# Second attention by groups of two head pairs, third attention's masks added on the vector engine

## What is computed

```python
def forgetting_attention(q, k, v, fcum):          # second attention, 16 heads of 64
    logits = einsum('bhtd,bhsd->bhts', q * scale, k) + fcum[:, :, :, None] - fcum[:, :, None, :]
    p = softmax(where(causal, logits, -inf), axis=-1)
    return einsum('bhts,bhsd->bhtd', p, v)

def sliding_window_gqa(q, k, v, sinks):           # third attention, 16 query heads, 2 key heads, window 128
    s = einsum('bqhgd,bkhd->bhgqk', q, k) * scale
    s = where(band, s, -inf)
    m = maximum(max(s, axis=-1), sink)
    p = exp(s - m)
    return einsum('bhgqk,bkhd->bqhgd', p / (sum(p, -1) + exp(sink - m)), v)
```

## Time and profile before

| | us |
|---|---|
| time before, median of 3 runs | 879.39 (879.27 to 879.51) |
| the profiled execution's own time | 879.21 |
| its span in the trace | 877.5 |
| PE busy | 864.6 (99%) |
| DVE busy | 676.3 (77%) |
| ACT busy | 515.6 (59%) |
| granted TensorE clock, mean | 0.999 |
| second attention, first logits to last outs | 350.76 to 425.03 |
| third attention, first logits to last outs | 657.5 to 723.4 |

### The profile page before, as it was taken

One profiled execution on the slowest core, in us unless ns is written; L12 is line 12 of the kernel. 1 busy time (PEld: TensorE's weight loads), 2 busy tenths in 40 slices (PEclk: granted clock), 3 DMA queues, 4 the chain that ended last, 5 costly groups with the idle time before them and its releaser, 6 DMA issues.

```text
span 877.5 us, 15051 instructions
## 1 busy us (share of the span) xinstructions
PE 864.6 (99%) x5840; PEld 754.4 (86%) x5840; DVE 676.3 (77%) x942; ACT 515.6 (59%) x754; POOL 50.3 (6%) x86
## 2 busy tenths in 40 slices
PE   8999999999999999999999999999999999999997
PEld 8999889888888899888798888888888778998885
DVE  5766469888888986656589888879878877699684
ACT  6655657765655774555486655656736757542452
POOL 3910000000000010000010000000100001000000
PEclk9999999999999999999999999999999999999999
DMA  8553425555455445242456365354353333562321
GB/s 295 205 174 139 145 96 204 204 199 206 170 193 201 154 164 218 103 144 96 145 204 239 145 217 207 151 204 179 110 209 138 104 140 121 189 212 89 133 97 49
DMA packets 21977, 144.64 MB, mean 165 GB/s; under 512 B 2831, under 2 KB 3103, under 8 KB 5280
## 3 DMA queue, kind: packets, MB, share of 16 engines
q1 hardware_dynamic: 20448, 139.47, 44.3%
q0 software_dynamic: 1328, 4.32, 1.5%
q10 hardware_dynamic: 144, 0.04, 0.0%
HBM read 142.78 MB, written 1.05 MB: 164 GB/s over the span
## 4 chain that ended last, share of the span: by engine, by line
PE 88%; DVE 6%; issue 2%; ACT 1%; DMA 1%; POOL 0%; SPq 0%; DVEq 0%; POOLq 0%; ACTq 0%
PE psC L1937 15%; PE psC L1848 12%; PE psC L1849 11%; PE psC L1850 11%; PE psC L1940 8%; PE psD L1848 5%; PE psD L1849 4%; PE psD L1850 4%; PE psC L1967 2%; PE psC L1969 2%; PE psC L1976 2%; PE psD L2224 2%; DVE arena L1257 2%; PE psD L2201 1%; PE psD L2213 1%
## 5 line engine op out<-in xcount | busy, mean ns | idle before, releaser
L1060 DVE TENSOR_TENSOR w_lo<-raw,w_hi 128x2048 fp32r<-128x2048 f32 x125 | 285.8, 2288 | 54.3 <-ACT w_hi L528 53.6
L528 ACT ACTIVATE w_hi<-raw 128x2048 fp32r<-128x2048 f32 x125 | 238.5, 1912 | 71.4 <-PE psC L1850 44.1
L1937 PE MATMUL psC<-xT,w_hi 128*128 128x512 f32 x640 | 200.8, 395 | 0.0
L1940 PEld LDWEIGHTS psC<-xT,w_lo 128*128 128x128 f32 x640 | 120.2, 188 | 28.3
L1940 PE MATMUL psC<-xT,w_lo 128*128 128x256 f32 x640 | 125.7, 278 | 0.0
L1937 PEld LDWEIGHTS psC<-xT,w_hi 128*128 128x128 f32 x640 | 98.6, 189 | 1.2
L1848 PE MATMUL psC<-xT,w_hi 128*128 128x256 f32 x320 | 92.1, 288 | 0.0
L1849 PE MATMUL psC<-xT,w_hi 128*128 128x256 f32 x320 | 90.5, 283 | 0.0
L1850 PE MATMUL psC<-xT,w_lo 128*128 128x256 f32 x320 | 90.5, 283 | 0.0
L1848 PE MATMUL psD<-w_hi,oT_hi 128*128 128x512 f32 x208 | 81.4, 391 | 0.6 <-DVE oT_lo L1271 0.6
L1849 PE MATMUL psD<-w_lo,oT_hi 128*128 128x512 f32 x208 | 81.0, 390 | 0.0
(11 more groups left out here) (327 smaller groups left out, 1522.3 us busy)
## 6 DMA issues: line engine op xcount, KB each, us to landing
raw<-stream SPq DMA_DIRECT2D x130, 1024.0 KB, 4.8
gbc<-post_g POOLq DMA_DIRECT2D x6, 512.0 KB, 4.5
h<-x_in SPq DMA_DIRECT2D x2, 512.0 KB, 4.5
raw<-stream SPq DMA_DIRECT2D x4, 256.0 KB, 6.3
out<-h SPq DMA_DIRECT2D x3, 256.0 KB, 2.0
arena<-b_in POOLq DMA_DIRECT2D x1, 640.0 KB, 5.9
out<-h SPq DMA_DIRECT2D x2, 128.0 KB, 2.0
pv<-pvec POOLq DMA_DIRECT2D x1, 176.0 KB, 5.0
```

Of the source, the lines that this page charges most:

```text
L528: nc.scalar.activation(w_hi[:, slot, :], raw[:, raw_slot, :], ACT.Copy).then_inc(hi_done, 1)
L1060: V.tensor_tensor(w_lo[:, slot, :], raw[:, raw_slot, :], w_hi[:, slot, :].bitcast(F32), ALU.subtract).then_inc(lo_done, 1)
L1937: MM(psC[:, up_bank(e, a), :], hi[:, k, a * P:a * P + P], xT[:, kk_, :, :].rearrange("p i t -> p (i t)"), start=(kk_ == 0), stop=False, sk ...
L1940: ins = MM(psC[:, up_bank(e, a), 0:T], lo[:, k, a * P:a * P + P], xT[:, kk_, 0, :], start=False, stop=(kk_ == KT - 1), skip_group_check=True)
```

## The change

In the second attention, PE's work is put in a row for groups g of two pairs: the forget sums and masks of both pairs (`forget_rows`), the outs of the group before (`outs_group`, now in banks that both pairs of a group share, by `group_out`), the logits of both pairs; and later both transposes. ACT and DVE follow: two maxima, two exponentials, two normalisations in a row, and one copy of 512 columns for the outs of a group where two of 256 were.

In the third attention the two mask matmuls of each pair are gone. The first L2224 matmul of a bank opens it (`start`). DVE reads logits from PSUM and the mask from SBUF, adds them, writes the sum to `pair_p` and takes the maximum, in four `tensor_tensor_reduce`. The exponentials read `pair_p` in place of PSUM.

```diff
@@ pair_exps (ACT)
-                if p >= 3:
+                if p >= 3 and w == 0:
                     act.wait_ge(s["turned"], p - 2)
                 for r in range(2):
                     i = 2 * p + r
                     for q, (a, b) in enumerate(((0, P), (P, 384))):
-                        ins = nc.scalar.activation(pair_p[p % 3][:, r, a:b], psD[:, 2 * (p % 2) + r, a:b], ACT.Exp,
+                        z = pair_p[p % 3][:, r, a:b] if w else psD[:, 2 * (p % 2) + r, a:b]
+                        ins = nc.scalar.activation(pair_p[p % 3][:, r, a:b], z, ACT.Exp,
                                                    bias=nmx[:, w, i, q:q + 1], accum_out=sums[:, w, i, q:q + 1])
@@ fox (ACT)
-                for p in range(H // 2):
-                    if p:
-                        probs_turned(0, p - 1)
-                    pair_exps(0, p)
-                    split_to(u0 + p + 5)
-                    if p:
-                        out_hi(p - 1)
-                    if p % 2 == 0:
-                        values_evac(p // 2)
-                probs_turned(0, 7)
-                out_hi(7)
+                for g in range(4):
+                    if g:
+                        out_hi(g - 1)
+                    pair_exps(0, 2 * g)
+                    pair_exps(0, 2 * g + 1)
+                    values_evac(g)
+                    split_to(u0 + 2 * g + 5)
+                    probs_turned(0, 2 * g)
+                    probs_turned(0, 2 * g + 1)
+                    split_to(u0 + 2 * g + 6)
+                out_hi(3)
@@ pair_max (DVE)
                 dve.wait_ge(s["logit"], p + 1)
-                V.tensor_reduce(mx[:, w, pair, 0], psD[:, at:at + 2, 0:P], AX.X, ALU.max)
-                settle(V.tensor_reduce(mx[:, w, pair, 1], psD[:, at:at + 2, P:384], AX.X, ALU.max))
                 if w == 0:
+                    V.tensor_reduce(mx[:, w, pair, 0], psD[:, at:at + 2, 0:P], AX.X, ALU.max)
+                    settle(V.tensor_reduce(mx[:, w, pair, 1], psD[:, at:at + 2, P:384], AX.X, ALU.max))
                     V.tensor_scalar(nmx[:, w, pair, :], mx[:, w, pair, :], -1.0, None, ALU.mult).then_inc(s["max"], 1)
                     return
+                if p >= 3:
+                    dve.wait_ge(s["turned"], p - 2)
+                for r in range(2):
+                    for q, (a, b) in enumerate(((0, P), (P, 384))):
+                        ins = V.tensor_tensor_reduce(pair_p[p % 3][:, r, a:b], psD[:, at + r, a:b], mask_window[:, a:b], 1.0, NEG,
+                                                     ALU.add, ALU.max, accum_out=mx[:, w, 2 * p + r, q:q + 1])
+                settle(ins)
@@ fox (DVE)
-                for p in range(H // 2):
-                    pair_max(0, p)
-                    split_to(u0 + p + 4)
-                    if p in (1, 3, 5):
-                        fox_keys((p + 1) // 2)
-                    normalize(0, p)
-                    if p:
-                        out_lo(p - 1)
+                for g in range(4):
+                    pair_max(0, 2 * g)
+                    pair_max(0, 2 * g + 1)
+                    if g:
+                        out_lo(g - 1)
+                    split_to(u0 + 2 * g + 4)
+                    normalize(0, 2 * g)
+                    normalize(0, 2 * g + 1)
+                    if g < 3:
+                        fox_keys(g + 1)
+                    split_to(u0 + 2 * g + 5)
                 split_to(u0 + 12)
-                out_lo(7)
+                out_lo(3)
@@ fox (PE)
+                def forget_rows(g):
+                    for p in (2 * g, 2 * g + 1):
+                        if g:
+                            pe.wait_ge(s["pT"], p - 1)
...
-                for p in range(7):
-                    g = p // 2
-                    logits(p)
-                    if p:
-                        turn_probs(0, p - 1)
...
+                for g in range(4):
+                    forget_rows(g)
+                    if g:
+                        outs_group(g - 1)
+                    logits(g)
+                    vals(g, 2)
+                    vals(g, 3)
+                    if g == 3:
                         break
...
+                    for i in range(4):
+                        keys(g + 1, i)
+                    turn_probs(0, 2 * g)
+                    turn_probs(0, 2 * g + 1)
+                    vals(g + 1, 0)
+                    vals(g + 1, 1)
+                out_ready(3)
@@ window, logits(p) (PE)
-                    for z in zs:
-                        MM(z[:, 0:384], ident_b[:, :], mask_window[:, :], start=True, stop=False, skip_group_check=True)
-                    pair_logits(zs, p, p // 4).then_inc(s["logit"], 1)
+                    pair_logits(zs, p, p // 4, True).then_inc(s["logit"], 1)
```

More of the change, by code:

```diff
@@ L803, in fox, with out_hi @@
                 u0 = U0["fox_kv"]
-                def out_hi(p):
-                    act.wait_ge(s["out"], p + 1)
-                    nc.scalar.activation(oT_hi[:, p, :], psD[:, 2 * (p % 2), 0:T], ACT.Copy).then_inc(s["ohi"], 1)
+                def out_hi(g):
+                    act.wait_ge(s["out"], g + 1)
+                    nc.scalar.activation(oT_hi[:, 2 * g:2 * g + 2, :].rearrange("p k t -> p (k t)"), group_out(g), ACT.Copy).then_inc(s["ohi"], 1)
                 def values_evac(g):
@@ L2207, in outs @@
                 pe.wait_ge(s["pT"], p + 1)
-                if w == 0 and p % 2 == 0:
-                    pe.wait_ge(chunk_freed_s, S_FREED[E0["fox_kv"] + p + 1])
                 o = [psD[DH * r:DH * r + DH, 2 * (p % 2), 0:T] for r in range(2)]
-                first = [(p // 4 if w else 2 * p + r) * DH for r in range(2)]
+                first = [(p // 4) * DH for r in range(2)]
                 for r in range(2):
@@ L2217, in outs, with pair_logits @@
                 ins.then_inc(s["out"], 1)
[L2219 removed]
+            def pair_logits(zs, p, keys, opens=False):
                 for a, b, q in ((0, P, slice(0, P)), (P, 384, slice(P, T))):
@@ L2223, in pair_logits @@
                         rows = slice(DH * r, DH * r + DH)
-                        ins = MM(z[:, a:b], qT[rows, p, q], kT[rows, keys, 0:b - a], start=False, stop=(a > 0), skip_group_check=True)
+                        ins = MM(z[:, a:b], qT[rows, p, q], kT[rows, keys, 0:b - a], start=(opens and a == 0), stop=(a > 0),
+                                 skip_group_check=True)
                 return ins
@@ L2340, in vals, with out_ready @@
                     tokens_piece(e0 + 2 * g + 1, u0 + 2 * g + 1, part)
[L2342 to L2357 removed]
+                def out_ready(g):
+                    pe.wait_ge(s["olo"], g)
@@ new lines, in logit_banks @@
+                def logit_banks(p):
+                    return [psD[:, 2 * (p % 2) + r, :] for r in range(2)]
+                def forget_rows(g):
+                    for p in (2 * g, 2 * g + 1):
+                        if g:
+                            pe.wait_ge(s["pT"], p - 1)
+                        for r, z in enumerate(logit_banks(p)):
+                            MM(z[:, 0:384], sel_r[:, 2 * p + r, :], neg_f_all, start=True, stop=False, skip_group_check=True)
+                    for p in (2 * g, 2 * g + 1):
+                        for z in logit_banks(p):
+                            MM(diagonal(z), ident_b[:, :], diagonal(mask_causal[:, :]), start=False, stop=False, skip_group_check=True)
@@ new lines, in logits, with outs_group @@
+                def logits(g):
+                    pe.wait_ge(chunk_freed_v, V_FREED[e0 + 2 * g])
+                    for p in (2 * g, 2 * g + 1):
+                        pair_logits(logit_banks(p), p, p).then_inc(s["logit"], 1)
+                def outs_group(g):
+                    pe.wait_ge(s["pT"], 2 * g + 2)
+                    pe.wait_ge(chunk_freed_s, S_FREED[e0 + 2 * g + 1])
+                    if g == 2:
+                        out_ready(1)
+                    for i in range(2):
+                        p, cols = 2 * g + i, group_out(g)[:, i * T:i * T + T]
+                        o = [cols[DH * r:DH * r + DH] for r in range(2)]
+                        first = [(2 * p + r) * DH for r in range(2)]
+                        for r in range(2):
+                            MM(o[r], vt[:, 0, first[r]:first[r] + DH], pair_pT[0][i][:, r, 0:T], start=(i == 0), stop=False, skip_group_check=True)
+                        for r in range(2):
+                            ins = MM(o[r][:, P:T], vt[:, 1, first[r]:first[r] + DH], pair_pT[0][i][:, r, T:384], start=False, stop=True,
+                                     skip_group_check=True)
+                    ins.then_inc(s["out"], 1)
```

52 lines of the change are left out of this document (9 added, 43 removed).

## The result

| | before | after |
|---|---|---|
| time, median (lowest to highest), us | 879.45 (879.27 to 879.51) | 874.0 (873.93 to 874.12) |
| ratio | | 0.9938 (0.9926 to 0.9951) |
| span of the profiled execution, us | 877.5 | 872.2 |
| second attention, us | 74.27 | 70.93 |
| third attention, first masks or logits to the end of the last outs, us | 65.82 | 64.12 |

What follows compares the result with a forecast made beforehand. PE, busy 99% of the span, bounds the kernel; DVE is nearest to taking over in the third attention. Second attention -3.4 plus third +0.3 gives -3.1 us: 876.1 from the profiled execution, stated as 876.3; range 874.0 to 878.7.

Steps and rivals of the forecast that it cites:

- Second attention, -3.4: Second attention, PE: grouping two pairs saves 0.86 us for each of four groups, 3.4 us; bounds 2.4 and 4.0.
- Third attention, PE's list, -2.6: Third attention, PE: without mask matmuls each of eight pairs loses 0.33 us, 2.6 us in all.
- D = 0.45: Third attention, DVE: extra time per pair for additions with maxima, 1.49 against 1.05 us; bounds 0.2 and 0.8.
- A: Third attention, ACT: extra time per pair for exponentials reading SBUF in place of PSUM, taken as 0.15 us.
- 5A: Third attention: ACT's extra 0.15 us counted five times, as normalising in pairs 1 to 5 waits for the exponentials.
- the forecast's formula: Third attention, chain DVE, ACT, DVE of pairs 0 to 6: shift = 7D + 5A - 3.6 = +0.3 us.
- 3.6: Third attention, taken off the shift: 0.33 earlier start, 2.55 DVE idle time, 0.7 estimated margins, in us.
- three places: Third attention, PE waits for DVE: third pair's logits (about 1.2 us), seventh pair's transposes, eighth pair's logits.
- The sign set for "hidden": Third attention: the stretch shrinking by 2 us or more would show the forecast wrong and the maxima hidden.
- The maxima stay hidden: Rival, third attention: write-outs free, chain roomy, PE's list alone decides; -6.0 us, 873.4; chance 0.08.
- A write-out that costs a whole small operation: Rival, third attention, DVE: each write-out of a maximum costs 0.16 us or more; in all -0.65, 878.7; chance 0.17.
- Half rate: Rival, third attention, DVE: additions at half rate add 0.8 us per pair; in all +2.5, 881.9; chance 0.08.

Runs made afterwards that it cites:

- The run with D = 0.52: The changed kernel with one more 256-column reduction (0.34 us) in each pair's maxima of the third attention; 876.41 us.
- At D = 0: The changed kernel without any window mask in the third attention, reductions and exponentials reading PSUM as before; 873.55 us.
- right split moved: Against the changed kernel with two projection pieces and end-of-stage DVE work reordered: DVE's 2.29 us split put ahead of a gating product; 874.62 us.

## Why the prediction was wrong, step by step

- **Second attention, -3.4:** right, -3.34, with the pieces as forecast (row of forget sums and masks 1.24 for 1.22, outs 1.45, logits 1.51, transposes 1.23 for 1.26). No wait, and 0.4 us of room for a forecast 0.5. This part alone gave the same 3.35.
- **Third attention, PE's list, -2.6:** right. The stage lost 1.70, less the entry ahead of it (0.08 to 0.10), and its waits cost 1.05 from start to start: 2.6 to 2.7 in all. The entry from the stream to the logits cost 0.09 to 0.10 (654.03 to 654.35 is 0.32, and a stream step of 512 columns 0.22 to 0.23).
- **D = 0.45: the step that failed.** It was the sum "Three of them and a last one with its settling (0.20) give 1.49". The additions were right, 1.11 for 1.08. The three write-outs, 0.07 each, cost nothing, and the settling 0.12 in place of 0.20. So D is 0.18, below even the lower bound of 0.2 (1.08 + 0.20 - 1.05 is 0.23: that lets the write-outs go but keeps the settling at 0.20). At seven times per stage, 0.27 too much makes 7 x 0.27 = 1.9 us, nearly the whole 2.3 that the forecast missed. The run with D = 0.52 shows that this multiplier is real: 6.7. The rest of the 2.3 is the 0.35 behind the stage, of which the forecast had nothing.
- **A:** 0.15 was the right size (a pair's exponentials take 1.78 from start to start in the changed kernel, 656.95 to 658.73, and 1.61 before, 660.42 to 662.03, so A is 0.17), but 5A was not: at this D it enters once (0.18 us in all). With D = 0.18 and A = 0.17 the forecast's formula gives 1.26 + 0.85 - 3.6 = -1.5, and the measured shift is -1.62. That agreement is partly luck, two errors that cancel: with A once the formula would give -2.2, so 5A is too large by 0.7 and 3.6 by some 0.55. The formula isn't one to trust at small D. There each wait is local. At D = 0 the wait before the seventh pair's transposes stays at 0.28, because from that pair's logits (702.83 in the changed kernel) to its normalisation DVE has its own list of work, a 2.28 us split among it, whatever came before: without the mask DVE sits idle for 0.58 ahead of that pair's maxima, and the wait is still there.
- **Where the waits are:** right in two of three places. The size at the first, 1.2 for a measured 0.50, is D's again: the forecast's own sum there, 2D + A - 0.33 + 0.66 - 0.2, gives 0.66 with the measured D and A. Of the 2.6 us some 1.0 came back, not all. The sign set for "hidden", 2 us or more off the stretch, was too wide: the stretch lost 1.7, and the forecast was wrong all the same.
- **The rivals.** "The maxima stay hidden" was half right: the write-outs are free, but the chain is not. A write-out that costs a whole small operation is excluded by the same rows. Half rate is excluded: the addition of 256 columns takes 0.35 from start to start and the one of 128 columns 0.21, the 0.34 and 0.20 worked out for full rate. By the Trainium skill, "Vector Engine (DVE) Microarchitecture Reference", section 7, `S2S2D2_STT` has half throughput with two sources in SBUF that aren't bf16. The operation of this trace (CUSTOM_DVE_ANT_0, 0.35 us for 256 columns) has one source in PSUM and a bf16 mask and runs at full rate, so it lies outside of that rule; no run here tests the rule itself.
- **What is left, 0.35 us.** In the kernel before, DVE begins the norm behind this stage 0.45 after ACT's row sum is there; in the changed one 0.10 after it. DVE timeline before:

```profile
727.05 0.69 DVE L1159 TENSOR_TENSOR hn<-psC,gbc 128x512 f32<-128x512 f32 x1 [2.21 <-ACT kT L570]
```

ACT timeline before, the first operation behind the row sum:

```profile
726.60 0.60 ACT L570 ACTIVATE kT<-psC 128x512 f32<-128x512 f32 x1
```

The same two of the changed kernel, DVE and ACT:

```profile
721.77 0.69 DVE L1160 TENSOR_TENSOR hn<-psC,gbc 128x512 f32<-128x512 f32 x1 [1.85 <-ACT kT L570]
```

```profile
721.67 0.60 ACT L570 ACTIVATE kT<-psC 128x512 f32<-128x512 f32 x1
```

The way from the end of the last outs to the next transposes is 6.24 us before and 5.89 after. With the second attention alone it is 5.96 and with the third alone 5.88. All thirteen other traces have 0.09 to 0.11, and only the one of before the 0.45, so neither part of the change takes it away by what it does. That it belongs to the kernel before and not to that one execution fits the times, where each part gave 0.3 to 0.4 more than its stage lost (3.8 for 3.35, 2.0 for 1.7), but isn't shown: there is one trace of the kernel before. What it comes from stays open.

## What to carry over

When a forecast multiplies a small term by the number of loop turns, that term is the one to bound, down to nothing as well: 0.27 us per pair was 1.9 us at the end. What DVE adds to each of seven turns counted nearly seven times (6.7) once PE waited at several places, and about four times (3.9) as long as each wait had its own late instruction. Before an instruction is put back because nobody waits for it, look at what stands behind its reader on that engine's list: a product put back by 2.2 us held up a copy that it has nothing to do with.

## What the runs showed of the hardware

- An operation of DVE that also gives a row maximum is two entries in the trace, and the second (0.08 us) starts together with the next operation. From start to start it costs nothing that the trace shows (0.21 and 0.35 with it, where 0.20 and 0.34 were worked out for the addition alone); only behind the last one do 0.12 us remain before an operation that reads the maxima. The Trainium skill, "VectorE: DVE Perf Modes", section "Two Vector instructions with no wait between them", says that such an operation is two instructions; the trace agrees on that.
- On PE, going to and fro between forget sums and masks costs 0.02 us in a group's row (1.26 against 1.24), a second visit to the logits and what stands ahead of them 0.41. Which kinds follow each other decides, not how often the kind changes; why, no run here tells.
- Code that is the same starts at other times in other traces: the forget sums between 350.51 and 351.34 us. Whether that is the kernel or the single execution, one trace of each kernel can't tell: one wait near the start of the program (PE's for a split by ACT, at 8.4 us in the changed kernel's trace) is 0.88 us there and 0.20 in the trace with the right split moved. For questions of some tenths the length of a stage is the measure, not the time of the kernel.
